# Attention of the sample in two units of 1024 keys a head, with a maximum for each unit

## What is computed

```python
def block_attention(q, k, v):
    ...
    scale = 1.0 / math.sqrt(dh)
    def one_block(qi):
        s = jnp.einsum('bqkgd,bskd->bkgqs', qi, k).astype(jnp.float32) * scale
        p = jax.nn.softmax(s, axis=-1).astype(v.dtype)
        return jnp.einsum('bkgqs,bskd->bqkgd', p, v)
...
q = axial_rope(rms_norm(q.reshape(b, n, ATTN_Q_HEADS, HEAD_DIM), q_norm), ang_row, ang_col)
```

## Time and profile before

| what | value |
|---|---|
| median of 3 runs | 5370.54 us (5363.93 to 5373.64) |
| the profiled execution, its time | 5393.33 us |
| its span, first to last instruction | 5391.5 us |
| granted TensorE clock, mean of the span | 0.928 |
| PE busy | 4389.7 us (81%) |
| DVE busy | 3113.5 us (58%) |
| ACT busy | 2088.0 us (39%) |
| POOL busy | 1069.9 us (20%) |

### The profile page before, as it was taken

One profiled execution on the slowest core, in us unless ns is written; L12 is line 12 of the kernel. 1 busy time (PEld: TensorE's weight loads), 2 busy tenths in 40 slices (PEclk: granted clock), 3 DMA queues, 4 the chain that ended last, 5 costly groups with the idle time before them and its releaser, 6 DMA issues. The chain is left out here.

```text
span 5391.5 us, 144326 instructions
## 1 busy us (share of the span) xinstructions
PE 4389.7 (81%) x61318; PEld 3987.2 (74%) x61318; DVE 3113.5 (58%) x6054; ACT 2088.0 (39%) x4040; POOL 1069.9 (20%) x829
## 2 busy tenths in 40 slices
PE   5878888886688876777777768871399999999998
PEld 5756666664687875766767766651399999999998
DVE  6867777775688883444444445556644444444443
ACT  3347777774455551111111112220143343434433
POOL 4432222222133342110001212210101011010100
PEclk9989999999899998998999889995599999999999
DMA  7810000000433322122121124430255555555553
GB/s 159 157 46 13 16 13 14 15 12 24 154 122 134 132 102 97 52 62 60 53 62 56 57 70 142 152 112 0 67 161 170 164 163 166 162 168 167 166 162 105
DMA packets 496719, 526.60 MB, mean 98 GB/s; under 512 B 74224, under 2 KB 434672, under 8 KB 496240
## 3 DMA queue, kind: packets, MB, share of 16 engines
q1 hardware_dynamic: 390256, 413.95, 24.0%
q10 hardware_dynamic: 92480, 62.93, 5.0%
q0 software_dynamic: 13504, 42.30, 3.5%
HBM read 372.12 MB, written 146.99 MB: 96 GB/s over the span
## 5 line engine op out<-in xcount | busy, mean ns | idle before, releaser
L2339 DVE TENSOR_TENSOR g_wlo<-g_raw,g_whi 128x2048 fp32r<-128x2048 f32 x192 | 439.1, 2287 | 129.8 <-ACT g_whi L2301 129.8
L615 PE MATMUL sapS<-KT,saq 128*128 128x512 f32 x1024 | 369.2, 443 | 122.9 <-ACT saprob L515 115.0
L2301 ACT ACTIVATE g_whi<-g_raw 128x2048 fp32r<-128x2048 f32 x192 | 366.0, 1906 | 245.4 <-DMA g_raw<-expert_w_gate 245.4
L568 DVE TENSOR_REDUCE samx<-sapS 128x1 f32<-128x512 f32 x512 | 352.8, 689 | 184.4 <-PE sapS L615 179.1
L2406 PE MATMUL g_pD<-g_whi,g_hh 128*128 128x256 f32 (+1 forms) x1536 | 437.9, 285 | 0.6
L2406 PE MATMUL g_pD<-g_whi,g_hl 128*128 128x256 f32 (+1 forms) x1536 | 429.3, 279 | 0.0
L2406 PE MATMUL g_pD<-g_wlo,g_hh 128*128 128x256 f32 (+1 forms) x1536 | 429.0, 279 | 0.0
L523 ACT ACTIVATE saph<-sapT 128x512 fp32r<-128x512 f32 x512 | 305.7, 598 | 226.4 <-PE sapT L630 219.7
L505 POOL TENSOR_SCALAR saprob<-saprob,sarden 128x2048 f32<-128x2048 f32 x128 | 254.5, 1988 | 655.4 <-DVE sarden L587 655.4
L1116 PE MATMUL c_pP<-c_xh,c_whi 128*128 128x258 f32 x1120 | 335.4, 299 | 46.5 <-DMA c_gup<-g_lora_up 27.9
L515 ACT ACTIVATE saprob<-sapS,sanm 128x512 f32<-128x512 f32 x512 | 345.9, 686 | 9.7 <-DVE sanm L574 9.6
(11 more groups left out here) (386 smaller groups left out, 13887.0 us busy)
## 6 DMA issues: line engine op xcount, KB each, us to landing
g_raw<-expert_w_gate SPq DMA_DIRECT2D x64, 1024.0 KB, 5.0
g_raw<-expert_w_up SPq DMA_DIRECT2D x64, 1024.0 KB, 5.1
g_raw<-expert_w_down SPq DMA_DIRECT2D x64, 1024.0 KB, 5.0
ops<-c_ops SPq DMA_DIRECT2D x40, 1024.0 KB, 4.0
d_bd<-ops SPq DMA_DIRECT2D x80, 512.0 KB, 4.0
c_xh<-xT_hi SPq DMA_DIRECT2D x10, 1032.0 KB, 5.6
c_xl<-xT_lo SPq DMA_DIRECT2D x10, 1032.0 KB, 8.4
x_in<-x SPq DMA_DIRECT2D x20, 512.0 KB, 7.9
```

Source lines behind the costliest of these rows:

```text
L568: ins = dve.tensor_reduce(mx[:, h % 2, k:k + 1], pS[k][:], AX.X, ALU.max)
L615: mm = pe.matmul(pS[k][:], q[:, h // GH, h % GH, :], KT[:, 2 * (h // GH) + p, key0 + k * 512:key0 + (k + 1) * 512], start=(p == 0), stop=( ...
L2301: act.activation(w_hi[:, Q % NBUF, :, :], raw[:, Q % NRAW, :, :], ACT.Copy).then_inc(s["g_hi"], 1)
L2339: dve.tensor_tensor(w_lo[:, Q % NBUF, :, :], raw[:, Q % NRAW, :, :], w_hi[:, Q % NBUF, :, :].bitcast(F32), ALU.subtract).then_inc(s["g_lo" ...
```

## The change

The scores of the sample are made in two units of 1024 keys, `pS[u]` being two banks each. Each unit has its own extreme and its own exponential, one instruction of 1024 columns each. The queries' gain is multiplied by -SCALE once in `attention_inputs`, so that the scores come out negated and scaled, and the extreme is a minimum that serves as the bias itself. Since the two units have different biases, the factor `share[u] = exp(nmin - nm[u])` is computed on ACT, the two sums are weighted with it, and POOL multiplies each half of the probabilities by its own rate, in two instructions of 1024 columns. The steps are laid out anew on all engines, `evacuate` of a pair moves one step later, and `qfree` is gone: the load of the next queries waits for the count of scores. The prompt (`NU == 1`) has one unit of 512 keys, and neither common minimum nor factor.

```diff
@@ attention_inputs, VectorE @@
             dve.wait_ge(s["a_gain"], 16 * (1 + NH))
+            dve.tensor_scalar(qk_gain[:, 0:QH, :], qk_gain[:, 0:QH, :], -SCALE, None, ALU.mult).then_inc(s["a_scale"], 1)
+            dve.wait_ge(s["a_scale"], 1)
@@ attention @@
+    NU = 2 if n_tiles > 4 else 1
+    NB = n_tiles // (4 * NU)
+    nb = NU * NB
+    UW = nk // NU
...
-        pS = [ps(f"{name}pS{k}") for k in range(nb)]
+        pS = [ps(f"{name}pS{u}", (P, NB, 512)) for u in range(NU)]
@@ SyncE @@
-                    sp.wait_ge(s["qfree"], KVH * t + g + 1)
+                    sp.wait_ge(s["score"], NU * (head(t, 0) + GH * (g + 1)))
@@ GpSimd @@
-                    pool.tensor_scalar(prob[:, h % 4, :], prob[:, h % 4, :], rden[:, h % 2:h % 2 + 1], 1.0, ALU.mult, ALU.mult).then_inc(s["norm"], 1)
+                    for u in range(NU):
+                        keys = slice(u * UW, (u + 1) * UW)
+                        pool.tensor_scalar(prob[:, h % 4, keys], prob[:, h % 4, keys], rate[:, h % 2, u:u + 1], 1.0, ALU.mult, ALU.mult).then_inc(s["norm"], 1)
@@ ScalarE @@
-            def exps(t, h, k):
+            def exps(t, h, u):
                 if live(t):
-                    if k == 0:
-                        act.wait_ge(s["nm"], head(t, h) + 1)
-                    act.activation(prob[:, h % 4, k * 512:(k + 1) * 512], pS[k][:], ACT.Exp, bias=nm[:, h % 2:h % 2 + 1],
-                                   scale=SCALE, accum_out=den[:, h % 2, k:k + 1]).then_inc(s["exp"], 1)
+                    act.wait_ge(s["nm"], NU * head(t, h) + u + 1)
+                    act.activation(prob[:, h % 4, u * UW:(u + 1) * UW], pS[u][:].rearrange("p k n -> p (k n)"), ACT.Exp, bias=nm[:, h % 2, u:u + 1],
+                                   scale=-1.0, accum_out=den[:, h % 2, u:u + 1]).then_inc(s["exp"], 1)
+
+            def shares(t, h):
+
+                if live(t):
+                    act.wait_ge(s["nmin"], head(t, h) + 1)
+                    act.activation(share[:, h % 2, :], nm[:, h % 2, :], ACT.Exp, bias=nmin[:, h % 2:h % 2 + 1], scale=-1.0).then_inc(s["share"], 1)
...
             def step(t, h):
-                before = back(t, h, 1)
-                exps(t, h, 0)
...
+                turning = back(t, h, 2)
+                for u in range(NU):
+                    for k in range(NB):
+                        high(*turning, NB * u + k)
+                    exps(t, h, u)
+                    if u == 0:
+                        evacuate(*back(t, h, 6))
+                if NU > 1:
+                    shares(t, h)
+                finish(*back(t, h, 6))
@@ VectorE @@
+            def top_of(t, h, u):
                 if live(t):
...
+                    dve.wait_ge(s["score"], NU * head(t, h) + u + 1)
+                    dve.tensor_reduce(nm[:, h % 2, u:u + 1], pS[u][:].rearrange("p k n -> p (k n)"), AX.X, ALU.min).then_inc(s["nm"], 1)
+
+            def common(t, h):
+                if live(t):
+                    dve.wait_ge(s["nm"], NU * (head(t, h) + 1))
+                    dve.tensor_reduce(nmin[:, h % 2:h % 2 + 1], nm[:, h % 2, :], AX.X, ALU.min).then_inc(s["nmin"], 1)
...
             def total(t, h):
                 if live(t):
+                    dve.wait_ge(s["exp"], NU * (head(t, h) + 1))
+                    if NU == 1:
+                        dve.reciprocal(rate[:, h % 2, :], den[:, h % 2, :]).then_inc(s["rate"], 1)
+                        return
+                    dve.wait_ge(s["share"], head(t, h) + 1)
+                    dve.tensor_tensor(part[:, h % 2, :], den[:, h % 2, :], share[:, h % 2, :], ALU.mult).then_inc(s["part"], 1)
...
+                    dve.tensor_reduce(dsum[:, h % 2:h % 2 + 1], part[:, h % 2, :], AX.X, ALU.add).then_inc(s["ds"], 1)
...
+                    dve.tensor_scalar(rate[:, h % 2, :], share[:, h % 2, :], rden[:, h % 2:h % 2 + 1], None, ALU.mult).then_inc(s["rate"], 1)
 
             def step(t, h):
...
+                turning = back(t, h, 2)
+                for u in range(NU):
+                    top_of(t, h, u)
+                    if u == 0:
+                        total(*back(t, h, 1))
+                    elif NU > 1:
+                        common(t, h)
+                    for k in range(NB):
+                        low(*turning, NB * u + k)
@@ TensorE @@
-                    if k == nb - 1 and h % GH == GH - 1:
-                        pe.wait_ge(s["score"], nb * (head(t, h) + 1))
-                        pe.sem_inc(s["qfree"], 1)
...
-                    if k == 0:
-                        pe.wait_ge(s["norm"], head(t, h) + 1)
+                    if k % NB == 0:
+                        pe.wait_ge(s["norm"], NU * head(t, h) + k // NB + 1)
...
+                for u in range(NU):
+                    score(t, h, u)
+                    for k in range(NB):
+                        turn(*turning, NB * u + k)
+                    for k in range(NB):
+                        product(*summing, NB * u + k)
```

More of the change, by code:

```diff
@@ L431, in attention @@
         q = sb(name + "q", [P, 2, GH, P], F32R)
-        mx = sb(name + "mx", [P, 2, nb])
-        top = sb(name + "top", [P, 2])
-        nm = sb(name + "nm", [P, 2])
+        nm = sb(name + "nm", [P, 2, NU])
+        nmin = sb(name + "nmin", [P, 2])
+        share = sb(name + "share", [P, 2, NU])
+        part = sb(name + "part", [P, 2, NU])
         prob = sb(name + "prob", [P, 4, nk])
-        den = sb(name + "den", [P, 2, nb])
+        den = sb(name + "den", [P, 2, NU])
         dsum = sb(name + "dsum", [P, 2])
         rden = sb(name + "rden", [P, 2])
+        rate = sb(name + "rate", [P, 2, NU])
         ph = sb(name + "ph", [P, 2, n_tiles, 2, P], F32R)
@@ L442, in attention @@
         o_out = sb(name + "o_out", [HD, 2, 2 * P])
-        pS = [ps(f"{name}pS{k}") for k in range(nb)]
+        pS = [ps(f"{name}pS{u}", (P, NB, 512)) for u in range(NU)]
         pT = [ps(f"{name}pT{k}") for k in range(2)]
         pO = [ps(f"{name}pO{k}") for k in range(2)]
-        s = sems("id q0 q1 qfree score mx nm exp ds rd norm tr hi lo pv osb fold oout st0 st1 seen", name + "_")
+        s = sems("id q0 q1 score nm nmin exp share part ds rd rate norm tr hi lo pv osb fold oout st0 st1 seen", name + "_")
         block = ctx.enter_context(nc.Block())
@@ L583, in total @@
                 if live(t):
-                    dve.wait_ge(s["exp"], nb * (head(t, h) + 1))
-                    dve.tensor_reduce(dsum[:, h % 2:h % 2 + 1], den[:, h % 2, :], AX.X, ALU.add).then_inc(s["ds"], 1)
+                    dve.wait_ge(s["exp"], NU * (head(t, h) + 1))
[4 more added lines that the diff above has]
+                    dve.tensor_tensor(part[:, h % 2, :], den[:, h % 2, :], share[:, h % 2, :], ALU.mult).then_inc(s["part"], 1)
+                    dve.wait_ge(s["part"], head(t, h) + 1)
+                    dve.tensor_reduce(dsum[:, h % 2:h % 2 + 1], part[:, h % 2, :], AX.X, ALU.add).then_inc(s["ds"], 1)
                     dve.wait_ge(s["ds"], head(t, h) + 1)
                     dve.reciprocal(rden[:, h % 2:h % 2 + 1], dsum[:, h % 2:h % 2 + 1]).then_inc(s["rd"], 1)
+                    dve.wait_ge(s["rd"], head(t, h) + 1)
+                    dve.tensor_scalar(rate[:, h % 2, :], share[:, h % 2, :], rden[:, h % 2:h % 2 + 1], None, ALU.mult).then_inc(s["rate"], 1)
             def step(t, h):
[L590 to L601, removed]
+                turning = back(t, h, 2)
[7 more added lines that the diff above has]
+                        low(*turning, NB * u + k)
             steps(dve, step)
@@ L606, in _, with score @@
         def _(pe):
-            def score(t, h, k):
+            def score(t, h, u):
                 if live(t):
-                    if k == 0 and h % GH == 0:
+                    if u == 0 and h % GH == 0:
                         pe.wait_ge(s[f"q{h // GH}"], 16 * (t + 1))
@@ L612, in score @@
                     if live(tb):
[L613 to L616, removed]
+                        pe.wait_ge(s["exp"], NU * head(tb, hb) + u + 1)
+                    for k in range(NB):
+                        keys = key0 + u * UW + k * 512
+                        for p in range(2):
+                            mm = pe.matmul(pS[u][:, k, :], q[:, h // GH, h % GH, :], KT[:, 2 * (h // GH) + p, keys:keys + 512],
+                                           start=(p == 0), stop=(p == 1))
                     mm.then_inc(s["score"], 1)
-                    if k == nb - 1 and h % GH == GH - 1:
-                        pe.wait_ge(s["score"], nb * (head(t, h) + 1))
-                        pe.sem_inc(s["qfree"], 1)
             def turn(t, h, k):
                 if live(t):
-                    if k == 0:
-                        pe.wait_ge(s["norm"], head(t, h) + 1)
+                    if k % NB == 0:
+                        pe.wait_ge(s["norm"], NU * head(t, h) + k // NB + 1)
                     if nb * h + k >= 2 or live(t - 1):
```

28 lines of the change are left out of this document (2 added, 26 removed).

## The result

The changed kernel takes 5250.7 us (median of 4 runs, 5241.84 to 5252.59) against 5369.76 us of the kernel before on the same chip: a ratio of 0.9776, 95% interval [0.9759, 0.9793]. That is 119 us less; 5248 was forecast.

What follows compares the result with a forecast made beforehand. No engine was full; the loop of scores, maxima and exponentials set the pace. Sample -127, prompt +4, gains +0.7 gave -122 us, so 5248 us, range 5240 to 5262, chance 0.51.

Steps and rivals of the forecast that it cites:

- The old loop: Sample's attention: scores, four maxima, their maximum and product, four exponentials, scores; 7.09 us a head, no longer binding after the change.
- The new pace: Sample: one chain through PE and DVE, turn 3 being transposes held by the second subtraction; mean 6.10 us a head.
- 5.77 us for a plain step: Sample step without fold: turn 3 starts at 4.41, then 0.36 and 1.0 us; the step ends at 5.77.
- 6.44 with a fold: Sample step containing a fold, which adds 0.67 us on PE: the step ends at 6.44.
- Two banks cost one slope: DVE's minimum over 1024 columns in two banks: 0.689 + 0.536 = 1.22 us, bounds 0.689 and 1.378.
- The rival of a double price: DVE's two-bank minimum costs twice one, 1.38 us, +0.16 in the chain; part of the dearer-chain rival, 5267 to 5285, chance 0.27.
- that of half rate: DVE's minimum over two banks runs at half rate, 2.3 us: +90 us, 5465 us, chance 0.03.
- The prompt, +4 us: Prompt's attention: evacuation behind the exponential delays fold and next score; +0.12 us a step, +4 us for 32.
- The gains' multiplication: Inputs: one operation of 512 columns ahead of the first tile, at most 0.7 us.
- The rule on the pipe: DVE: the next operation waits until the pipe is empty, removing 0.08 us overlaps at four places; DVE alone 6.2 to 6.3.
- PE is the bound: Rival for the sample: PE waits for nothing, 5.98 us a head; 5233 us, chance 0.15.
- DVE alone is the bound: Sample, within the dearer-chain rival (chance 0.27): without overlap of small operations or handoffs, DVE alone needs 6.25 us a head.

Runs made afterwards that it cites:

- e2: Changed kernel with both sample exponentials taking the common minimum as bias, so waiting for both units: sample's stretch 890.9 us, 110.1 more.
- e5: Changed kernel with each unit's minimum made as two of 512 columns and a third over the two: sample's stretch 822.2 us, 41.4 more.
- e3: Changed kernel with weighting, sum, reciprocal and rates on DVE behind the two subtractions: sample's stretch 753.0 us, 27.8 less; whole 0.9744 of the kernel before.
- e8: Changed kernel with all 16 products of a step at its end, not eight behind each unit's transposes: sample's stretch 897.2 us, 116.4 more.
- e6: Changed kernel with each unit's exponential made as two of 512 columns: sample's stretch 780.6 us against 780.8.
- e1: Kernel before with only qfree removed, so PE no longer waits for its own scores: sample's stretch 890.3 us, 9.6 less; whole ratio 0.9977.
- e4: Changed kernel with the prompt's evacuation put back ahead of the exponential: prompt's stretch 102.0 us against 106.6, sample 779.0.

## Why the prediction was right, point by point

- *The old loop goes with the separate biases.* Shown by e2: +110 us without them.
- *The new pace is a chain of score, minimum, rates, two subtractions, turn 3 and products, and PE's order covers the rest.* Shown from three sides: longer minima +41 us (e5), the rates off the chain -28 us (e3), the products off their place +116 us (e8), each within 2 us of the expected range. The wait ahead of turn 3 is 0.22 us a head, and 0.13 was in the sum.
- *5.77 us for a plain step*: measured 5.77 between POOL's starts, partly by terms that cancel. (Between the first scores, the prediction's own mark, the two steps are 5.87 and 6.43, since the plain one begins behind a fold; the mean is the same.) Scores take 0.93 rather than 1.02, and the reduction starts 1.13 after them rather than 1.20; the rates take 0.71 from the first small operation to the subtraction, not 0.66, since the rates' own instruction takes 0.23.
- *6.44 with a fold*: measured 6.53. The fold costs its 0.67, and the scores behind it start to transposes in 1.03 rather than 0.93. It is the term that was too small, 0.09 us at 64 steps, 6 us in all; the mean is 6.15 and not 6.10, the sample's gain -122 and not -127.
- *Two banks cost one slope*: 1.221 us, forecast 1.22. The rival of a double price and that of half rate are out. The wide exponential at 1.116 is hidden, as e6 shows from the other side.
- *`qfree` is inside the sum*: the 7.09 us of the kernel before hold it, and alone it is worth 10 us in the sample (e1). The prediction gave no number for it.
- *The prompt, +4 us*: measured -0.8 by the marks. The pair of steps is 2.52 + 3.43 = 5.95 us, forecast 6.14, before 5.90 on average: the mechanism (the evacuation behind the exponential holds the fold, and that the next score) is right, as e4 shows by taking it back, 0.57 us a pair; PE's wait ahead of the fold grew from 0.55 to 1.2 us, as forecast. The pair was mis-sized by 0.19, 3 us in 16 pairs, because the score starts 0.58 and not 0.66 after the fold, and the exponential 0.06 earlier. And the stage's first five steps, before any fold, became 1.1 us shorter (16.0 against 17.1), which the forecast left out. The half clock lasted 16 us in the one trace and 17 in the other, so these two can be compared. The same code for the prompt in e2, e5, e6 and e8, with half clock until 27 to 36 us, took 110 to 112 us by the marks in place of 106.6: against such an execution the forecast would have looked right, for another reason.
- *The gains' multiplication* took 0.43 us.
- *The rule on the pipe.* The small operation starts at 607.18, 1.14 us after a reduction of 1.23 began, so 0.09 before its recorded end: what the forecast took from the short operations holds for the wide reduction too. The Trainium skill, "VectorE: DVE Perf Modes", section "The DRAIN you can't avoid", would by the sentence that the prediction weighed have it start after that end, and there the trace disagrees; the same section adds that a next operation that is not held starts earlier, which the prediction left out.
- *PE is the bound*, the first rival: not so, though the windows say 100 of 100. In e3 a plain step takes 5.60, and of its second eight transposes only 0.06 us is wait; DVE has then no idle time in it either, and which of the two sets the pace of e3 is open. Its mean of 5.92 a head lies below the 5.98 that the prediction gave PE alone, so that figure was too high.
- *DVE alone is the bound*, priced in the second rival at 6.25 a head: not so. e3 has the same instructions on DVE in another order and takes 5.92 a head, so DVE needs no more than that. But it was close: in the changed kernel DVE waits for scores 62 times, once in two heads, behind a fold (0.84 us ahead of the reduction at 612.57), and between two such waits it stands nowhere idle for more than some 0.1 us.

The sum agreed in the end with the median to 3 us, closer than its terms, and that is luck: it had the sample's gain 5 us too large and a loss of 4 us in the prompt that did not come, and the two errors cancel.

## What to carry to other kernels

When a softmax waits for the maximum of a whole row before the first bank comes free, split the row into units with a maximum each and pay with a factor at the end; but give PE work between a unit's transposes and the next unit's: without it the handoff took the whole gain back here (e8). Put small operations that nobody waits for behind those whose result frees a bank, and look for each shape apart how soon its result is wanted: what was hidden by a whole step in the sample was wanted at once in the prompt. Compare such kernels by marks around the stage, and PE by its matmuls in a window, not by its busy share.

## What was not expected of the hardware

- A group of matmuls is shown busy across a wait of 0.22 us: PE at 100 of 100 us did 670 matmuls in one kernel and 697 in another, at a clock of 1.00 in both.
- After the barrier ahead of the prompt PE starts at a granted clock of 0.50, its lower level, and the time until it is at 1.00 differs between executions of the same code: it rises some 16 us after the stage's first score in the changed kernel, 27 us in e6 and 36 us in e5, whose prompt code is the same. From 10 to 30 us into the stage the changed kernel is at 0.86 in the window shown above, e5 at 0.50:

```profile
1186.00:1206.00 20.00, 16.20 (x57) 12.40 (x55) 8.03 (x17) 7.43 (x18) 3.80 (x6) 0.50 0.09 30
```

  First to last score of the prompt took 93.5 us in the one and 99.1 in the other. Why it differs was not tried.
- A `TENSOR_SCALAR` of two columns with a column as its factor took 0.23 us, the other small operations 0.15 to 0.16.
